# Two stacks of mixers on one core: the dummy matmuls at the layer norms and at the pre-norm of the first stack are left out

## What is computed

```python
def first_block(x, ...):
    h = x
    for l in range(DEPTH):                       # DEPTH = 2
        proj = h @ w_in[l]
        ...
        mixed = jnp.concatenate([nsa_mixer(...), gla_mixer(...), pool_mixer(...)], axis=-1)
        h = layer_norm(DEEPNORM_ALPHA * h + mixed @ w_out[l], ln1_g[l], ln1_b[l])
        ff = jnp.square(jax.nn.relu(h @ w_up[l])) @ w_down[l]
        h = layer_norm(DEEPNORM_ALPHA * h + ff, ln2_g[l], ln2_b[l])
    return h

def layer_norm(x, g, b):
    xf = x.astype(jnp.float32)
    mu = jnp.mean(xf, -1, keepdims=True)
    var = jnp.mean(jnp.square(xf - mu), -1, keepdims=True)
    return ((xf - mu) * lax.rsqrt(var + LN_EPS)).astype(x.dtype) * g + b

# second stack, for each of its two layers, over meta tokens and x
h = h + rms_norm(mixer(rms_norm(h, pre), *mix), post)
h = h + rms_norm(conv_ffn(rms_norm(h, f_pre), w_up, c_w, c_b, w_down), f_post)
```

## Time and profile before

| | |
|---|---|
| median of 3 runs | 1420.05 us (1418.11 to 1420.32) |
| profiled execution | 1418.43 us, its span 1416.4 us |
| mean granted clock of TensorE | 0.998 |
| busy share of the span | PE 97%, PEld 83%, DVE 74%, ACT 59%, POOL 39% |
| HBM read | 232.62 MB, 165 GB/s over the span |

### The profile page before, as it was taken

One profiled execution on the slowest core, in us unless ns is written; L12 is line 12 of the kernel. 1 busy time (PEld: TensorE's weight loads), 2 busy tenths in 40 slices (PEclk: granted clock), 3 DMA queues, 4 the chain that ended last, 5 costly groups with the idle time before them and its releaser, 6 DMA issues.

```text
span 1416.4 us, 31773 instructions
## 1 busy us (share of the span) xinstructions
PE 1380.2 (97%) x13555; PEld 1180.2 (83%) x13555; DVE 1047.6 (74%) x1390; ACT 837.5 (59%) x1289; POOL 553.7 (39%) x445
## 2 busy tenths in 40 slices
PE   9999999999999999999899999999999999999997
PEld 7778888888778888887678888888788787888887
DVE  5787986557697884567778898756868865798853
ACT  6585554337574544447786655544776777576552
POOL 0134995122056992224210575603213211356620
PEclk9999999999999999999999999999999999999999
DMA  9534466554333665534336365552643333466551
GB/s 372 181 120 149 153 211 212 195 179 150 105 136 120 238 209 203 184 105 164 119 120 226 122 220 186 187 190 91 209 149 120 101 124 106 163 224 218 182 181 31
DMA packets 36876, 235.71 MB, mean 166 GB/s; under 512 B 4736, under 2 KB 7808, under 8 KB 9984
## 3 DMA queue, kind: packets, MB, share of 16 engines
q1 hardware_dynamic: 36736, 233.68, 48.0%
HBM read 232.62 MB, written 1.05 MB: 165 GB/s over the span
## 4 chain that ended last, share of the span: by engine, by line
PE 78%; DVE 12%; ACT 6%; issue 3%; POOL 1%; DMA 0%; ACTq 0%; DVEq 0%; POOLq 0%
PE psum L730 22%; PE psum L731 22%; PE psum L732 22%; DVE low L2371 4%; ACT high L1712 2%; PE psum L815 1%; PE psum L817 1%; PE psum L816 1%; ACT m L2109 1%; PE psum L989 1%; PE psum L936 1%; POOL m L3157 1%; DVE arena L2792 1%; DVE m L2860 1%; POOL h L3159 1%
## 5 line engine op out<-in xcount | busy, mean ns | idle before, releaser
L2371 DVE SCALAR_TENSOR_TENSOR low<-raw,high 128x2048 f16<-128x2048 f32 (+4 forms) x246 | 531.9, 2169 | 198.8 <-ACT high L1712 198.5
L730 PE MATMUL psum<-u,high 128*128 128x256 f16 (+3 forms) x2024 | 557.0, 275 | 3.5 <-DVE arena L2792 3.5
L732 PE MATMUL psum<-u,low 128*128 128x256 f16 (+3 forms) x2024 | 556.8, 275 | 0.0
L731 PE MATMUL psum<-u,high 128*128 128x256 f16 (+3 forms) x2024 | 556.7, 275 | 0.0
L1712 ACT ACTIVATE high<-raw 128x2048 f16<-128x2048 f32 (+3 forms) x249 | 420.6, 1693 | 119.4 <-PE psum L732 88.6
L730 PE MATMUL psum<-arena,high 128*128 128x256 f16 (+2 forms) x1112 | 305.5, 275 | 4.4 <-issue 1.6
L731 PE MATMUL psum<-arena,high 128*128 128x256 f16 (+2 forms) x1112 | 305.5, 275 | 0.0
L732 PE MATMUL psum<-arena,low 128*128 128x256 f16 (+2 forms) x1112 | 305.3, 275 | 0.0
L730 PEld LDWEIGHTS psum<-u,high 128*128 128x128 f16 (+1 forms) x2024 | 198.1, 98 | 36.9 <-issue 7.6
L731 PEld LDWEIGHTS psum<-u,high 128*128 128x128 f16 (+1 forms) x2024 | 198.3, 98 | 29.0 <-issue 0.7
L732 PEld LDWEIGHTS psum<-u,low 128*128 128x128 f16 (+1 forms) x2024 | 198.2, 98 | 28.3
(11 more groups left out here) (364 smaller groups left out, 1837.0 us busy)
## 6 DMA issues: line engine op xcount, KB each, us to landing
raw<-stream SPq DMA_DIRECT2D x208, 1024.0 KB, 4.8
raw<-stream SPq DMA_DIRECT2D x8, 768.0 KB, 4.2
raw<-stream SPq DMA_DIRECT2D x3, 896.0 KB, 4.8
raw<-stream SPq DMA_DIRECT2D x3, 512.0 KB, 3.4
con<-consts SPq DMA_DIRECT2D x1, 1437.0 KB, 14.3
h<-x_t SPq DMA_DIRECT2D x2, 512.0 KB, 6.3
misc<-small SPq DMA_DIRECT2D x1, 512.0 KB, 15.1
out_t<-h SPq DMA_DIRECT2D x1, 512.0 KB, 3.6
```

What stands on the lines that cost most here:

```text
L730: pe.matmul(out, w_hi, x[0], start=start, stop=False)
L731: pe.matmul(out, w_hi, x[1], start=False, stop=False)
L732: return pe.matmul(out, w_lo, x[0], start=False, stop=stop)
L2371: tell(dve.scalar_tensor_tensor(low[:, at:at + w], raw[:, off:off + w], W_SCALE, high[:, at:at + w], ALU.mult, ALU.subtract), split_ready ...
```

## The change

`keep_awake` is taken out, with the argument `awake` of `abreast` and `product` that led to it, and the call in `pre_norm`. That is 138 dummies. The wait for the first bank ahead of the dummies goes too; the same wait follows in the loop over the pairs and stays. The 40 dummies at the opening stay.

```diff
-            def keep_awake(b, times):
-
-                for _ in range(times):
-                    pe.matmul(bank(b, 0, 2 * P), ident16, C("ident", 0, P).bitcast(BF16), start=True, stop=True)
-
-            def abreast(name, ahead, rhs, ready, n, order, awake=0, x_high=None):
+            def abreast(name, ahead, rhs, ready, n, order, x_high=None):
 
                 prod = products[name]
-                if awake:
-                    bank_free(prod["first"])
-                    keep_awake(BANK[prod["first"]], awake)
                 for step in prod["steps"][:ahead]:
                     await_slot(step[0])
                     for j in step[1]:
...
-                    abreast(f"in1_{l}", 2, x_at, operand_ready(3 * l), S, range(KT), AWAKE_1, operand_high(3 * l))
+                    abreast(f"in1_{l}", 2, x_at, operand_ready(3 * l), S, range(KT), x_high=operand_high(3 * l))
...
-                product(f"up1_{l}", x_at, operand_ready(3 * l + 2), S, awake=AWAKE_1, x_high=operand_high(3 * l + 2))
+                product(f"up1_{l}", x_at, operand_ready(3 * l + 2), S, x_high=operand_high(3 * l + 2))
...
                 norm = 2 * DEPTH
-                keep_awake(BANK[products["in_g"]["first"]], AWAKE_G)
                 for k in range(KT):
...
-                abreast("in_g", 2, x_at, operand_ready(6), T, range(KT), AWAKE_G, operand_high(6))
+                abreast("in_g", 2, x_at, operand_ready(6), T, range(KT), x_high=operand_high(6))
...
-AWAKE_0, AWAKE_1, AWAKE_G = 40, 30, 24
+AWAKE_0 = 40
```

More of the change, by code:

```diff
@@ L896, in last_pair_in_halves, with product @@
                 tile_sums(n, KT - 2, 1)
-            def product(name, rhs, ready, n, after=None, late=None, order=None, pairs=2, begun=0, last_pair=None, awake=0, x_high=None):
+            def product(name, rhs, ready, n, after=None, late=None, order=None, pairs=2, begun=0, last_pair=None, x_high=None):
                 prod = products[name]
@@ L906, in product @@
                 if ahead and not begun:
-                    abreast(name, ahead, rhs, ready, n, ks_in, awake, x_high)
+                    abreast(name, ahead, rhs, ready, n, ks_in, x_high)
                 if ahead and after:
```

## The result

The median of four runs is 1430.45 us (1428.35 to 1433.64) against 1419.24 us (1418.11 to 1420.32) for four runs of the kernel before; the ratio is 1.0072, 95% interval [1.0051, 1.0093]. The forecast was 1423.8 us, between 1419.8 and 1427.0. The sign was right; the size was 11 us where 3.75 had been forecast, and the measured time lies outside the range.

The account below looks back on a forecast made before the run. It took TensorE, with 78% of the last chain, as the bound. The profiled 1418.43 us plus 3.75 us (2.5 falls x 1.5) gave 1422.2, plus 1.6 to the median 1423.8 us; range 1419.8 to 1427.0.

Parts of the forecast that it names:

- The sign: Whole kernel: the change makes it slower, chance 0.60 (same 0.37, faster 0.03).
- The dummies' own time: At the norms, pre-norm and in_g: removing the dummies' own time gains 0; at in_g less than 0.1 us is left.
- The mechanism: At the uncovered idle gaps: the clock falls to half speed, with matmul starts 0.22 us apart behind them.
- The price of one fall: Behind an uncovered gap: 3.4 us at the low clock lose 1.5 us, range 1.0 to 1.7.
- four gaps with a chance of about 0.6 each are two or three falls: Three norms and the gap ahead of the pre-norm's sums: 2.5 x 1.5 = 3.75 us.
- the 2.15 us of idleness that left the clock up: Idle stretch behind dense matmuls in the profile of before: the clock read 1.00 afterwards.
- rival (d): Faster: the fall at 1178 us may be missed by another timing of the program, -1.5 us; chance 0.03.
- rival (c): Pre-norm: low clock lasts over the sums (3.93 us more), then start of in_g low too (1.7); 1430 us; chance 0.05.
- I had excluded a fall ahead of in_g: The 2.1 us idle between the pre-norm's fp32 sums and in_g: no fall taken there.
- I let nothing be absorbed: Later TensorE waits (longest 1.9 us, L1087): they move along, so the whole loss reaches the end.
- rival (a): All four gaps bring a fall, as the page's rule gives: 4 x 1.5 = 6.0 us, 1426.1 us; chance 0.12.

Follow-up runs that it names:

- e6: Kernel before with only the 24 dummies ahead of in_g left out; 1421.84 us, ratio 1.0014.
- e12: e9 with the dummies at all three norms left out; 1425.44 us, 8.6 us over e9, ratio to the kernel before 1.0028.
- e15: e9 with the dummies left out at the second norm alone; 1418.46 us, 1.6 us over e9.
- e3: Kernel before with only the dummies of the pre-norm and ahead of in_g left out; 1424.5 us, ratio 1.0023.
- e4: Kernel before with all 138 dummies kept, each on a 32x32 corner of the array instead of 128x128; 1422.71 us, ratio 1.0024.
- e5: The kernel after, unchanged, run and profiled again; 1429.88 us, ratio to the kernel before 1.0075.
- e9: Kernel before plus dummies in four gaps: 16 ahead of the GLA states' wait (both layers), 18 in in_m, 14 ahead of out_m; 1416.85 us; the quiet base.
- e2: Kernel before with only the dummies at the three norms left out; 1423.51 us, ratio 1.0034.
- e17: e9 with the dummies left out at the first and second norm; 1425.39 us, 8.5 us over e9, ratio to the kernel before 1.0023.
- e7: Kernel before with only the 24 dummies ahead of the pre-norm's sums left out; 1423.47 us, ratio 1.002.
- e13: e9 with the dummies of the pre-norm and ahead of in_g left out; 1419.89 us, 3.0 us over e9, ratio to the kernel before 1.0000.
- e14: e9 with 8 dummies at each norm for 30, and 6 at each pre-norm place for 24; 1422.16 us, ratio to the kernel before 1.0026.
- e16: e9 with the dummies left out at the first and third norm; 1420.75 us, 3.9 us over e9.
- e11: The kernel after with the added blocks of e9; 1426.75 us, 9.9 us over e9, ratio to the kernel before 1.0043.
- e8: Kernel before with the same added blocks as e9, three of four one step too late; 1423.33 us, ratio 1.0031.
- e10: Kernel before with half the dummies: 15 at each norm, 12 in the pre-norm and 12 ahead of in_g; 1420.18 us, ratio 1.0002.

## Why the prediction was wrong

**Right.** The dummies' own time was worth nothing: TensorE was idle for 3.44, 3.44, 3.45, 3.35 and 2.10 us, as worked out. e6, where the clock held at in_g, shows that term by itself: from the start of the sums L751 came 0.36 us sooner than before (6.03 for 6.39 us) and the L730 that needs the low part 0.02 us sooner (7.76 for 7.78). The mechanism was the clock, at half speed behind the gaps, with starts 0.21 us apart (143.22, 143.43). The price of one fall, 1.5 us with 1.0 to 1.7, was nearly right: the ladder of before has steps of 1.65 us.

**The step that failed first is the sum, "four gaps with a chance of about 0.6 each are two or three falls".** Of 20 norms left bare and profiled, 19 fell (the second norm of e12 held, and by the times the second norm alone, e15, lost nothing in four of 11 runs). The fourth gap, ahead of the pre-norm's sums, fell in four of the six profiles in which it was bare, near my 0.6. That makes 3.5 falls, 5.8 us at 1.65 each (an estimate), where I had 3.75. The row on which I leaned, the 2.15 us of idleness that left the clock up, was one draw: the same gap fell in after (1016), e3, e4, e5 and e6. I had read one profile as if a place either falls or doesn't. The three other gaps outside the norms (55, 361 and 1177 us) were draws as well; e9 shows that before's median holds two such falls. I gave them to rival (d) as "1.5 us, more isn't in the profile"; they are 3.3.

**The second is one fall, one price.** A low stretch can last twice as long: 6.8 us at a norm in e2 (the third) and e17 (the second), and at the pre-norm. At the pre-norm the low clock lasted 6.8 us in after, e3 and e7 (3.4 in e13), over the fp32 sums, which took 6.87 us for 3.93 in after: +2.9. That is rival (c)'s first half, to which I gave 0.05; its second half, in_g starting low too, came in after and e3. I had excluded a fall ahead of in_g. That (c) named 1430 us, what after takes, is luck: e5 took 1428.57 us with no fall in the pre-norm. On the quiet base the pre-norm costs 3.0 us (e13) where the sum had 0.6 x 1.5.

**The third is what was not in the sum at all.** I followed the delays only through the waits and not into the light stretches behind them. With the first two norms bare, the mixers of the second layer fell as well (e17: +8.5 us for two gaps, in its profile 4.4 at the norms and 4.3 behind 388 us; e15, the second norm alone, had +1.6). That this pair of norms costs more than one fall each is shown; that the delay is what brings the fall behind it is only argued. No run delayed the mixers without a fall, e14 fell at both norms and held there, and in e16 the same work of the first layer fell with nothing ahead of it.

**A fourth, smaller, went the other way.** I let nothing be absorbed. The wait that I named (L1087) moved along whole, 1.88 us, but that of L1208 took in 1.05 us of after's loss, and 0.6 us of e17's.

**The sum as measured**, on the base of 1416.85 us: e12 + e13 = 8.6 + 3.0 = 11.6 us against 9.9 for all at once (e11); in means it is 7.5 + 3.2 = 10.7 against 9.3. With runs that spread over 5 to 9 us in each, neither difference is clear of the spread. Added to before's two falls, 1420.1 + 9.9 = 1430.0, which is what after takes. The forecast's 3.75 us is a little over a third of it. The page's rule (Trainium skill, "TensorE: Matmul & The Clock Gate", "Why this matters for your kernels"), taken as rival (a) with 1426.1 us, was nearer than my estimate and still 4 us short: it speaks of idle gaps, and the 4.3 us behind 388 in e17 came with TensorE busy. Its remark in "What's actually happening", that the monitor runs freely, agrees with the runs: one unchanged kernel gave 143 times on a ladder of five steps.

**Open.** Why e2, with all three norms bare, had a median 3.5 us over before and no low clock near 390 in its profile, while e12 had 8.6 over its base: with 9 and 10 runs that spread over 11 and 9 us, the medians don't settle it. Nor does the third norm show in e12 (8.6 us, three norms) against e17 (8.5 us, two). What decides in an execution whether a bare stretch falls, and for how long, was not isolated.

## What to carry to other kernels

A stretch of TensorE that may cost a fall is to be priced by many executions, not by one trace: look whether the times of one kernel stand on a ladder, and cover the gaps until the ladder is gone. A block of dummies belongs directly ahead of the wait and has to be shorter than it; one step too late it costs its full length (e8 against e9, with the same 64 dummies: 6.5 us in the median, and 4.9 us between two profiles without a fall). It need not fill the gap: half the block held the clock as well as the whole to within 2 us (e10), a quarter didn't (e14).

## What the runs showed of the hardware that was not expected

The clock can stay low while TensorE is busy without a break: 9.9 us at 0.50 in e17 over small and fp32 matmuls, and as long over the same work of the first layer in e16 (77.0 to 87.2 us); in the pre-norm it stayed low over nearly all of the fp32 sums. Dummies of 32x32 held the clock in some gaps and not in others (e4), although they take as long as full ones (0.27 us each). And the time of one unchanged kernel moves by 7 us (1416.7 to 1423.8), nearly all of it through this; with the four gaps covered, ten of 11 runs lie within 0.5 us.
